# The block inverse of a gated delta rule: larger blocks on VectorE, fewer product levels on TensorE

## The chip, the core and the metric

The kernel runs on one core of one Trainium2 chip. The time is that of one execution on the device, in microseconds, as the median of three runs. A profiled execution was taken beside them; its span is the time from its first to its last instruction.

## What is computed

One layer of a hybrid decoder for 256 tokens of width 1024, all in float32:

```python
h = rms_norm(x, norm_mix)
x = x + token_mixer(h, ...)      # w_in, gated delta rule and mLSTM, w_up_*, gates, w_out
h = rms_norm(x, norm_ffn)
x = x + moe_ffn(h, ...)          # top 4 of 32 experts, clamped SwiGLU
out = rms_norm(x, norm_final)
```

The change is in the gated delta rule, with 4 heads of width 128. The reference solves in chunks of 64 tokens; the kernel takes chunks of 128, so 4 heads x 2 chunks make 8 systems:

```python
lower = where(strict, einsum("id,jd->ij", kb, k) * decay, 0.0)
sol = triangular_solve(lower + eye, rhs, lower=True, unit_diagonal=True)
u_local, w_state = sol[..., :dv], sol[..., dv:]
```

The kernel does not solve, it forms the inverse of each unit triangular 128x128 matrix (lower + eye) and multiplies with it.

## The kernel before

The mixer comes first, the experts (MoE) behind it. SyncE issues nearly all weight transfers. Into a ring of places it fetches first 24 pieces of w_in, 1 MB each, then 4 pieces of w_up and 4 of w_out, each when TensorE has finished with the piece that lay there (piece_done), and then 192 pieces of 2 MB of expert weights, each when one of ten places is free (double_done).

TensorE runs a list written out by hand. `proj(j)` multiplies piece j of w_in with the turned input (32 records in the trace, since a float32 product is two records) into bank 6 or 7 by turns. Between the proj calls stand small products of the two mixer branches. Pieces 0 to 9 go through a causal convolution, `conv(j)` on VectorE, which ends in conv_done; proj(j + 2) waits for that, since it writes the same bank. Piece 10 and those behind it are taken by ScalarE (proj_taken). Each of the engines works its list in its own order and waits on semaphores; the function `link` on VectorE makes the next instruction wait for the one just issued.

The inverse is made so. VectorE forms `lt` (the transposed strict triangle, one 128x128 block for each system, 8 side by side) and signals lt_ready. GpSimd then copies the diagonal blocks of size BASE x BASE to device memory (base_in_copy) and from there back so that each block lies within one partition: with BASE = 16 these are 64 blocks on 64 partitions. VectorE inverts them column by column, all at once, with two instructions a column (`solve_base`), and writes the inverse and its transpose (base_out). GpSimd brings both back through device memory into the diagonals of `inv` and `invT`, 128x128 blocks filled with zeros before (base_loaded). Then come three levels, for blocks of 16, 32 and 64, each of which joins two inverted blocks into one of twice the size. For a level VectorE makes `ltm`, `lt` times a mask that keeps (with the sign changed) only the blocks that the level needs (`mask_level`); TensorE multiplies it with `inv` (`level_t1`), VectorE copies the result to `t1`, TensorE forms P and Q (`level_pq`: invT with t1, t1 with invT), and VectorE adds them to `inv` and `invT` (`level_dve`). The last level leaves P out, as only `invT` is used behind it.

Around this, VectorE's list is: conv(8), solve_base, conv(9), four products into `pt` (pt_ready; the mLSTM weights), mask_level(0), three casts of the expert bias `bgu`, four products of v with beta into `vb` (vb_ready), two subtractions and more casts for the bias, one product into `kd0` (kd_ready), then mlstm_rows (which writes `om`, a part of `hn`, and signals ml_sums_taken) and the levels. TensorE's is: proj(8), proj(9), the mLSTM products of k and q, proj(10), proj(11), the transposes of v, proj(12), a wait for vb_ready, the transposes of k, proj(13), the mLSTM sums, proj(14), a wait for kd_ready, and from there the levels' batches, one between each two proj calls up to proj(20). Then come the rest of the mixer, the router and the experts.

Of the kernel before, what the change touches and what calls it, by code (L numbers as in the profile page):

```python
# [24 lines left out]
ALU = mybir.AluOpType  # L25
# [3 lines left out]
P = 128  # L29
# [5 lines left out]
HALF = 512  # L35
# [8 lines left out]
def decoder_layer(nc, x, norm_mix, w_in, gdn_conv, gdn_a_log, gdn_dt_bias, gdn_norm, ml_conv,  # L44
# [5 lines left out]
    H = gdn_a_log.shape[1]  # L50
    DH = gdn_norm.shape[1]
    T = S // P
# [47 lines left out]
    for g in range(N_GROUPS):  # L100
        a, b = GROUPS[g]
# [20 lines left out]
    with ExitStack() as ctx:  # L122
# [5 lines left out]
        def sem(name):  # L128
            if name not in sems:
                sems[name] = ctx.enter_context(nc.semaphore(name))  # L130
            return sems[name]
# [9 lines left out]
        def mixer_only(n):  # L141
            at_early[0] += n
            assert at_early[0] <= 2 * PIECE
            return early[:, at_early[0] - n:at_early[0]]
# [3 lines left out]
        hn = sb("hn", [P, T, D])  # L148
# [12 lines left out]
        lt = head4(late[3])  # L161
        ltm = sb("ltm", [P, H, T, P])
        inv, invT = head4(late[4]), head4(late[5])
        t1 = head4(late[6])
# [12 lines left out]
        triu = mixer_only(P)  # L177
        striu = sb("striu", [P, P])
        ones = sb("ones", [P, P])
        BASE = 16  # L180
        NB = P // BASE
        LEVELS = [16, 32, 64]
        level = mixer_only(len(LEVELS) * P).rearrange("p (m i) -> p m i", i=P)
        prm = sb("prm", [96, P])
        prmT = sb("prmT", [P, 96])
        ffn_rows = sb("ffn_rows", [P, KC])
        base_in = mixer_only(BASE * BASE)[0:NB * H * T, :].rearrange("q (p f) -> q p f", p=BASE)
        base_out = mixer_only(2 * BASE * BASE)[0:NB * H * T, :].rearrange("q (i r c) -> q i r c", i=2, r=BASE)
        base_step = mixer_only(BASE * BASE // 4)[0:NB * H * T, :]
        base_in_copy = nc.dram_tensor("base_in_copy", [NB, H * T, BASE, BASE], F32).ap()  # L190
        base_out_copy = nc.dram_tensor("base_out_copy", [NB, H * T, 2, BASE, BASE], F32).ap()
# [335 lines left out]
                    pool.dma_start(diagonal(v, b), base_out_copy[b, :, i].rearrange("a r c -> r a c")).then_inc(sem("base_loaded"), 16)  # L527

        TABLES = 4


        @block.tensor
        def _(pe):
            def proj(j):

                dst = B[6 + j % 2]
                landed(pe, j)
                if 2 <= j <= CONV_PIECES + 1:
                    pe.wait_ge(sem("conv_done"), 2 * (j - 1))
                if j >= CONV_PIECES + 2:  # L540
                    pe.wait_ge(sem("proj_taken"), j - 1 - CONV_PIECES)
                w = slot3(j % RING, KC)
                for c in range(2):
                    for k in range(KC):
                        if NAT_FIRST <= j < GATE_FIRST:
                            lhs, rhs = hT[:, k, c * P:(c + 1) * P], w[:, k, :]
                        else:
                            lhs, rhs = w[:, k, c * P:(c + 1) * P], hT[:, k, :]
                        mm = pe.matmul(dst[:, c * S:(c + 1) * S], lhs, rhs, start=(k == 0), stop=(k == KC - 1))  # L549
                mm.then_inc(sem("piece_done"), 1)  # L550
# [8 lines left out]
            def per_head(banks, signal, product):  # L559

                for h in range(H):
                    for t in range(T):
                        i = h * T + t
                        lhs, rhs = product(h, t)
                        mm = pe.matmul(B[banks[i // 4]][:, (i % 4) * P:(i % 4 + 1) * P], lhs, rhs, start=True, stop=True)  # L565
                        if i % 4 == 3:
                            mm.then_inc(sem(signal), 1)
# [87 lines left out]
            def level_t1(m):  # L655
                pe.wait_ge(sem("level_ready"), m + 1)
                per_head((0, 1), "t1_done", lambda h, t: (ltm[:, h, t, :], inv[:, h, t, :]))

            def level_pq(m):
                pe.wait_ge(sem("t1_ready"), m + 1)  # L660
                if m < len(LEVELS) - 1:
                    per_head((2, 3), "p_done", lambda h, t: (invT[:, h, t, :], t1[:, h, t, :]))
                per_head((4, 5), "q_done", lambda h, t: (t1[:, h, t, :], invT[:, h, t, :]))

            proj(9)

# [30 lines left out]
            mm.then_inc(sem("ml_sums_done"), 1)  # L697
            proj(14)
            pe.wait_ge(sem("kd_ready"), 1)
            pe.wait_ge(sem("base_loaded"), 16 + 16 * 2 * NB)  # L700
            level_t1(0)
            proj(15)
            pe.wait_ge(sem("ml_sums_taken"), 1)
            level_pq(0)
            proj(16)
            level_t1(1)
            proj(17)
            level_pq(1)
            proj(18)
            level_t1(2)  # L710
            proj(19)
            level_pq(2)
            proj(20)

            pe.wait_ge(sem("om_ready"), 1)
            pe.wait_ge(sem("inv_ready"), 2)
            transposes([om[:, t, h * P:(h + 1) * P] for h in range(H) for t in range(T)], (2, 3), "om_turned")
            proj(21)
            pe.wait_ge(sem("inv_ready"), 3)
            chunk_products(0, "u0_done", lambda h: (invT[:, h, 0, :], vb[:, h, 0, :]))  # L720
            proj(22)
            pe.wait_ge(sem("u0_ready"), 1)
# [358 lines left out]
        def _(dve):  # L1081
            steps = [0]

            def link(ins):

                steps[0] += 1
                ins.then_inc(sem("dve_step"), 1)
                dve.wait_ge(sem("dve_step"), steps[0])
# [146 lines left out]
            def mask_level(m):  # L1235
                dve.tensor_tensor(m8, l8, bc(level[:, m, :].unsqueeze(1), [P, H * T, P]), ALU.mult).then_inc(sem("level_ready"), 1)
# [12 lines left out]
            link(dve.tensor_tensor(v, v, bc(triu[:, :].unsqueeze(1).unsqueeze(1), [P, H, 2, P]), ALU.mult))  # L1249
            conv(8)  # L1250

            def solve_base():

                lower = base_out[:, 0]
                link(dve.memset(base_out[:, :, :, :], 0.0))
                link(dve.memset(base_out[:, 0].rearrange("q r c -> q (r c)")[:, 0:BASE * BASE:BASE + 1], 1.0))
                dve.wait_ge(sem("base_loaded"), 16)
                for j in range(BASE - 1):
                    shape = [NB * H * T, BASE - 1 - j, j + 1]
                    step = base_step[:, 0:shape[1] * shape[2]].rearrange("q (r c) -> q r c", c=j + 1)  # L1260
                    link(dve.tensor_tensor(step, bc(base_in[:, j, j + 1:BASE].unsqueeze(2), shape),
                                           bc(lower[:, j:j + 1, 0:j + 1], shape), ALU.mult))
                    v = lower[:, j + 1:BASE, 0:j + 1]
                    link(dve.tensor_tensor(v, v, step, ALU.subtract))
                dve.tensor_copy(base_out[:, 1], lower.rearrange("q r c -> q c r")).then_inc(sem("base_solved"), 1)

            solve_base()
            conv(9)
            for h in range(H):
                dve.wait_ge(sem("ml_kq_done"), h + 1)  # L1270
                w = pt[:, h, :, :].rearrange("p b i -> p (b i)")
                dve.scalar_tensor_tensor(out=w, in0=B[2 + h][:, 0:3 * P], scalar=QS, in1=w, op0=ALU.mult,
                                         op1=ALU.mult).then_inc(sem("pt_ready"), 1)
# [6 lines left out]
            def level_dve(m):  # L1280
                for b in range(2):
                    dve.wait_ge(sem("t1_done"), 2 * m + b + 1)
                    ins = dve.tensor_copy(t18[:, b * HALF:(b + 1) * HALF], B[b])
                    if b == 0:
                        link(ins)
                ins.then_inc(sem("t1_ready"), 1)
                if m < len(LEVELS) - 1:
                    for b in range(2):
                        dve.wait_ge(sem("p_done"), 2 * m + b + 1)
                        v = invf[:, b * HALF:(b + 1) * HALF]  # L1290
                        link(dve.tensor_tensor(v, v, B[2 + b], ALU.add))
                for b in range(2):
                    dve.wait_ge(sem("q_done"), 2 * m + b + 1)
                    v = invTf[:, b * HALF:(b + 1) * HALF]
                    ins = dve.tensor_tensor(v, v, B[4 + b], ALU.add)
                    if b == 0:
                        link(ins)
                ins.then_inc(sem("inv_ready"), 1)
                if m < len(LEVELS) - 1:
                    dve.wait_ge(sem("inv_ready"), m + 1)  # L1300
                    mask_level(m + 1)

            def split_bias(part):

# [47 lines left out]
            def head_norm(o, scratch, t, col):  # L1352
# [2 lines left out]
                link(dve.tensor_tensor(scratch, v, v, ALU.mult))  # L1355
                link(dve.tensor_reduce(ss[:, col:col + H], scratch.rearrange("p (h i) -> p h i", h=H), AX.X, ALU.add))

            mlstm_rows()
            dve.wait_ge(sem("base_loaded"), 16 + 16 * 2 * NB)
            level_dve(0)  # L1360
            dve.wait_ge(sem("ml_sums_taken"), 1)
            for t in range(T):
                head_norm(om, scr, t, t * H)
            dve.tensor_scalar(ss[:, :], ss[:, :], 1.0 / DH, NORM_EPS, ALU.mult, ALU.add).then_inc(sem("ml_ms_ready"), 1)
            level_dve(1)
            dve.wait_ge(sem("ml_root"), 1)
            dve.wait_ge(sem("tail_params"), 16 * 5)

# [12 lines left out]
            dve.wait_ge(sem("proj_taken"), 6)  # L1381
            for t in range(T):
                gated(om, t, mnorm[:, :].rearrange("p (h i) -> p h i", h=H), mo_s, "om_ready", t == T - 1)
            level_dve(2)
            for b in range(2):
                dve.wait_ge(sem("om_turned"), b + 1)
                ins = dve.tensor_copy(cvm[:, 2 * b:2 * b + 2, :].rearrange("p h i -> p (h i)"), B[2 + b])
# [578 lines left out]
```

## Time and profile before

| what | us |
|---|---|
| median of 3 runs | 1230.27 |
| lowest and highest | 1226.4, 1232.22 |
| the profiled execution, its own time | 1226.06 |
| its span | 1223.8 |
| TensorE busy | 1158.8 |
| VectorE busy | 310.6 |
| ScalarE busy | 128.8 |

How to read it: the share of busy time is a mean over a mixer of about 300 us and an expert part of about 900 us that are limited by different things. The chain of waits follows back from the last instruction what released it. A row of a timeline is a run of like instructions of an engine: when it starts, how long it lasts, how many there are, and in square brackets how long the engine had been idle and who released it. The records of TensorE overlap a little in a timeline; the chain gives the time from start to start.

### The profile page before, as it was taken

How to read it: one execution, taken by the hardware profiler on the slowest of the kernel's cores; microseconds unless marked ns; L12 is line 12 of the kernel's file. 1: busy time of each engine (PE TensorE's matmuls, PEld its weight loads, DVE VectorE, ACT ScalarE, POOL GpSimd, SP SyncE). 2: the span in 40 equal slices, each digit the busy share in tenths (PEclk: the TensorE clock that was granted, in tenths of full speed). 3: DMA queues.
4: the chain of work that ended last, by engine and by line, in shares of the span. 5: the costliest groups of instructions: out<-in, count | busy, mean ns of one | idle time of the engine just before them, and what ended most of it. 6: DMA issues, size and time to landing. Idle time of an engine off the chain costs nothing.

```text
span 1223.8 us, 13499 instructions
## 1 busy us (share of the span) xinstructions
PE 1158.8 (95%) x5701; PEld 598.0 (49%) x5701; DVE 310.6 (25%) x705; ACT 128.8 (11%) x216; POOL 21.3 (2%) x57
## 2 busy tenths in 40 slices
PE   8989999999999999999989898999999998899996
PEld 7878998876434343433424342434434343334342
DVE  2688432345321120201102020202112020202021
ACT  3551101001000000000000000000000000000001
POOL 1003000000000000000000000000000000000000
PEclk9999999999999999999999999999999999999999
DMA  9944334385999999999999999999999999999994
GB/s 257 383 129 142 111 103 138 110 372 211 381 428 417 428 428 428 428 427 428 427 428 427 428 427 428 427 428 427 427 427 428 428 428 428 428 427 428 428 420 194
DMA packets 63644, 443.21 MB, mean 362 GB/s; under 512 B 8772, under 2 KB 33968, under 8 KB 38016
## 3 DMA queue, kind: packets, MB, share of 16 engines
q1 hardware_dynamic: 57968, 438.38, 86.9%
q10 hardware_dynamic: 4416, 1.99, 0.7%
q0 software_dynamic: 1200, 1.98, 0.5%
q8 instruction: 46, 0.75, 0.2%
q14 instruction: 14, 0.11, 0.0%
HBM read 441.07 MB, written 1.26 MB: 361 GB/s over the span
## 4 chain that ended last, share of the span: by engine, by line
PE 62%; DMA 32%; DVE 3%; SPq 1%; issue 1%; ACT 1%; POOL 0%; ACTq 0%; DVEq 0%
DMA ring<-in_w_down 30%; PE bank L844 22%; PE bank L887 13%; PE bank L549 11%; PE bank L824 3%; PE bank L780 2%; PE bank L926 2%; PE bank L565 1%; SPq L439 1%; PE bank L750 1%; PE bank L739 1%; PE bank L836 1%; DMA ring<-rows_copy 1%; PE bank L901 1%; PE bank L572 1%
## 5 line engine op out<-in xcount | busy, mean ns | idle before, releaser
L844 PE MATMUL bank<-ring,cvg 128*64 128x512 f32 x2112 | 461.9, 593 | 9.5 <-DMA ring<-in_w_gate_up 9.2
L844 PEld LDWEIGHTS bank<-ring,cvg 128*64 128x64 f32 x2112 | 151.3, 137 | 300.8 <-issue 274.5
L887 PE MATMUL bank<-ring,cvg 128*64 128x512 f32 x1024 | 236.5, 618 | 29.4 <-DMA ring<-in_w_down 29.4
L1516 DVE TENSOR_SCALAR cvm<-bank 128x512 f32<-128x512 f32 x33 | 22.8, 692 | 651.0 <-PE bank L844 651.0
L549 PE MATMUL bank<-ring 128*128 128x256 f32 x768 | 169.7, 380 | 4.1 <-DVE cvm L1154 4.1
L887 PEld LDWEIGHTS bank<-ring,cvg 128*64 128x64 f32 x1024 | 80.0, 142 | 183.7 <-issue 183.7
L549 PEld LDWEIGHTS bank<-ring 128*128 128x128 f32 x768 | 144.4, 190 | 23.5 <-ACT ring L1826 3.5
L1896 ACT ACTIVATE cvm<-cvm 128x512 f32<-128x512 f32 x33 | 20.8, 629 | 497.4 <-DVE cvm L1516 497.4
L824 PEld LDWEIGHTS bank<-ltm,hn 128*128 128x128 f32 x544 | 66.6, 196 | 7.3 <-issue 7.1
L824 PE MATMUL bank<-ltm,hn 128*128 128x128 f32 x544 | 66.9, 281 | 0.0
L926 PE MATMUL bank<-vb,ltm 128*128 128x512 f32 x128 | 57.7, 593 | 0.0
L1905 ACT ACTIVATE vb<-bank 128x512 f32<-128x512 f32 x32 | 17.4, 594 | 244.3 <-PE bank L887 244.3
L1506 DVE TENSOR_TENSOR cvg<-bank,ffn_rows 128x512 f32<-128x512 f32 x34 | 23.4, 691 | 63.3 <-PE bank L824 63.2
L926 PEld LDWEIGHTS bank<-vb,ltm 128*128 128x128 f32 x128 | 23.2, 192 | 23.8 <-issue 23.8
L1900 ACT ACTIVATE cvg<-bank 128x512 f32<-128x512 f32 x32 | 18.9, 589 | 99.2 <-PE bank L911 99.2
L780 PE MATMUL bank<-ring 128*128 128x512 f32 x64 | 28.0, 593 | 0.0
L911 PEld LDWEIGHTS bank<-ident,cvg 128*128 128x128 f32 x132 | 18.4, 207 | 13.4 <-issue 13.0
L1521 DVE SCALAR_TENSOR_TENSOR cvm<-cvm 128x512 f32<-128x512 f32 x33 | 22.9, 693 | 4.2 <-DVE cvm L1517 0.9
L1525 DVE TENSOR_TENSOR cvg<-cvm 128x512 f32<-128x512 f32 x33 | 22.8, 692 | 1.1
L911 PE MATMUL bank<-ident,cvg 128*128 128x128 f32 x132 | 23.0, 296 | 0.0
L1517 DVE TENSOR_SCALAR cvm<-bank 128x512 f32<-128x512 f32 x33 | 22.5, 680 | 0.0
L836 PE MATMUL bank<-bgu,picked 96*64 96x512 bf16 x132 | 20.4, 386 | 0.0
(328 smaller groups left out, 550.8 us busy)
## 6 DMA issues: line engine op xcount, KB each, us to landing
ring<-in_w_gate_up SPq DMA_DIRECT2D x128, 2048.0 KB, 31.5
ring<-in_w_down SPq DMA_DIRECT2D x58, 2048.0 KB, 35.0
ring<-in_w_in SPq DMA_DIRECT2D x24, 1024.0 KB, 6.7
ring<-in_w_down SPq DMA_DIRECT2D x12, 1024.0 KB, 34.0
ring<-in_w_out SPq DMA_DIRECT2D x4, 1024.0 KB, 4.9
ring<-in_w_up_ml SPq DMA_DIRECT2D x2, 1024.0 KB, 5.1
ring<-in_w_up_gdn SPq DMA_DIRECT2D x2, 1024.0 KB, 5.0
xs<-in_x SPq DMA_DIRECT2D x2, 512.0 KB, 4.4
```

Of the source, the lines that this page charges most:

```text
L549: mm = pe.matmul(dst[:, c * S:(c + 1) * S], lhs, rhs, start=(k == 0), stop=(k == KC - 1))
L780: return pe.matmul(B[2 * t + n], gate_g[:, kk, t * P:(t + 1) * P], slot3((OUT_FIRST + i) % RING, 2)[:, k, n * HALF:(n + 1) * HALF], start= ...
L824: mm = pe.matmul(B[6 + b][:, (k % 4) * P:(k % 4 + 1) * P], by_row[:, k // 2, k % 2, :], onehot[:, t, :], start=(t == 0), stop=(t == T - 1))
L836: pe.matmul(B[4 + half][side * SLOTS:(side + 1) * SLOTS, :], picked[:, e, :], bgu[:, at:at + HALF], start=True, stop=False, skip_group_che ...
L844: mm = pe.matmul(B[4 + half][side * SLOTS:(side + 1) * SLOTS, :], xT[:, k, e * SLOTS:(e + 1) * SLOTS], w[:, (k % 2) * PIECE + at:(k % 2) * ...
L887: mm = pe.matmul(B[6 + half][e * SLOTS:(e + 1) * SLOTS, :], actT[:, e, at:at + SLOTS], by_block(double(of[e]), 4)[:, j, half * HALF:(half ...
L911: mm = pe.transpose(B[to][:, c * P:(c + 1) * P], by_row[:, c, :], ident[:, :])
L926: mm = pe.matmul(B[2 * t + half], scat[:, t, :], ysb[:, half * HALF:(half + 1) * HALF], start=False, stop=False, skip_group_check=True)
L1506: dve.tensor_tensor(xT[:, 4 * b:4 * b + 4, :], B[6 + b].rearrange("p (k s) -> p k s", k=4), bc(ffn_rows[:, 4 * b:4 * b + 4].unsqueeze(2), ...
L1516: dve.tensor_scalar(g2, both[:, :, :, 0], SWIGLU_LIMIT, None, ALU.min).then_inc(sem("glu_g_ready"), 1)
L1521: dve.scalar_tensor_tensor(out=glu_u, in0=glu_u, scalar=1.0, in1=glu_g, op0=ALU.add, op1=ALU.mult).then_inc(sem("glu_u_ready"), 1)
L1525: dve.tensor_tensor(act[:, e, :], glu_u, glu_s, ALU.mult).then_inc(sem("act_ready"), 1)
```

## The change

The diagonal blocks are now 32x32, so there are 32 of them on 32 partitions with 31 columns to work; the working arrays base_out and base_in lie in `hn`, which is free there. Only the level for blocks of 32 stays as it was, with its P and Q. The last level, for blocks of 64, is written as 64x64 quarters: the lower left quarter is `lt` times `inv` with 64 rows and 64 columns, without a mask, and its Q goes with a factor of -1 straight into a quarter of `invT`. On VectorE, conv(9) is put between columns 11 and 12 of the solve. On TensorE, proj(15) and proj(16) stand ahead of the first level. VectorE waits for base_loaded ahead of mlstm_rows. GpSimd issues 4 copies out and 8 back instead of 8 and 16.

```diff
-        BASE = 16
+        BASE = 32
-        LEVELS = [16, 32, 64]
+        LEVELS = [32]
-        base_in = mixer_only(BASE * BASE)[...]
-        base_out = mixer_only(2 * BASE * BASE)[...]
+        base_out = hn[0:NB * H * T, :, :].rearrange("q i (r c) -> q i r c", r=BASE)
+        base_in = base_out[:, 1]
...
             def level_pq(m):
                 pe.wait_ge(sem("t1_ready"), m + 1)
-                if m < len(LEVELS) - 1:
-                    per_head((2, 3), "p_done", lambda h, t: (invT[:, h, t, :], t1[:, h, t, :]))
+                per_head((2, 3), "p_done", lambda h, t: (invT[:, h, t, :], t1[:, h, t, :]))
                 per_head((4, 5), "q_done", lambda h, t: (t1[:, h, t, :], invT[:, h, t, :]))
+            def last_t1():
+                pe.wait_ge(sem("inv_ready"), len(LEVELS))
+                for i in range(H * T):
+                    h, t = i // T, i % T
+                    mm = pe.matmul(B[0][UPPER, i * HP:(i + 1) * HP], lt[LOWER, h, t, UPPER], inv[LOWER, h, t, LOWER],
+                                   start=True, stop=True)
+                mm.then_inc(sem("t1_done"), 1)
+            def last_q():
+                pe.wait_ge(sem("t1_ready"), len(LEVELS) + 1)
+                for i in range(H * T):
+                    h, t = i // T, i % T
+                    mm = pe.matmul(B[4][LOWER, i * HP:(i + 1) * HP], t1[UPPER, h, t, LOWER], invT[UPPER, h, t, UPPER],
+                                   start=True, stop=True)
+                mm.then_inc(sem("q_done"), 1)
...
             pe.wait_ge(sem("kd_ready"), 1)
+            proj(15)
+            proj(16)
             pe.wait_ge(sem("base_loaded"), 16 + 16 * 2 * NB)
             level_t1(0)
-            proj(15)
+            proj(17)
             pe.wait_ge(sem("ml_sums_taken"), 1)
             level_pq(0)
-            proj(16)
-            level_t1(1)
...
             proj(18)
-            level_t1(2)
+            last_t1()
             proj(19)
-            level_pq(2)
+            last_q()
             proj(20)
...
-            solve_base()
+            open_base()
+            solve_base(0, 12)
             conv(9)
+            solve_base(12, BASE - 1)
+            dve.tensor_copy(base_out[:, 1], lower.rearrange("q r c -> q c r")).then_inc(sem("base_solved"), 1)
...
+            def last_level():
+                side = lambda v, rows, cols: v.rearrange("p h t i -> p (h t) i")[rows, :, cols]
+                turned = B[0].rearrange("p (a i) -> p a i", i=HP)[UPPER, :, :]
+                dve.wait_ge(sem("t1_done"), 2 * len(LEVELS) + 1)
+                dve.tensor_copy(side(t1, UPPER, LOWER), turned).then_inc(sem("t1_ready"), 1)
+                dve.wait_ge(sem("q_done"), 2 * len(LEVELS) + 1)
+                dve.tensor_scalar(side(invT, LOWER, UPPER), B[4].rearrange("p (a i) -> p a i", i=HP)[LOWER, :, :], -1.0, None,
+                                  ALU.mult).then_inc(sem("inv_ready"), 1)
...
+            dve.wait_ge(sem("base_loaded"), 16 + 16 * 2 * NB)
             mlstm_rows()
-            dve.wait_ge(sem("base_loaded"), 16 + 16 * 2 * NB)
-            level_dve(0)
...
-            level_dve(1)
+            level_dve(0)
...
-            level_dve(2)
+            last_level()
```

VectorE's list from the end of the solve on, before (an instruction reads: line, operation, what it writes from what, size; L1264 is the subtraction of the solve, L1154 conv(9), L1272 pt, L1236 the mask, L1307 the casts, L1325 vb):

```order
L1264 TENSOR_TENSOR ring<-ring 64x15
L1265 COPY ring<-ring 64x256
L1154 SCALAR_TENSOR_TENSOR cvg<-bank,prmT,cvg 128x255
...
L1154 SCALAR_TENSOR_TENSOR cvg<-bank,prmT,cvg 128x253
L1272 SCALAR_TENSOR_TENSOR ring<-bank,ring 128x384 x4
L1236 TENSOR_TENSOR ltm<-ring 128x1024
L1307 CAST bgu<-ring 32x2048 x3
L1325 TENSOR_TENSOR vb<-bank,rowsrc 128x256 x4
L1315 TENSOR_TENSOR ring<-ring,bgu 32x2048 x2
L1331 TENSOR_TENSOR kd<-bank,ex 128x512
```

And after, where the same lines are L1284, L1290, L1170, L1294, L1252, L1335 and L1353; the first row is the last one of column 11:

```order
L1284 TENSOR_TENSOR hn<-hn,ring 32x20x12
L1170 SCALAR_TENSOR_TENSOR cvg<-bank,prmT,cvg 128x255
...
L1170 SCALAR_TENSOR_TENSOR cvg<-bank,prmT,cvg 128x253
L1281 TENSOR_TENSOR ring<-hn 32x247
...
L1284 TENSOR_TENSOR hn<-hn,ring 32x31
L1290 COPY hn<-hn 32x1024
L1294 SCALAR_TENSOR_TENSOR ring<-bank,ring 128x384 x4
L1252 TENSOR_TENSOR ltm<-ring 128x1024
L1335 CAST bgu<-ring 32x2048 x3
L1353 TENSOR_TENSOR vb<-bank,rowsrc 128x256 x4
```

conv(9) stood behind the whole solve and stands now behind its first 12 columns; 19 columns and the copy stand between conv(9) and all that followed it.

TensorE's list from the sums of the mLSTM branch (L695) to the transposes of om, before (L549 is a proj, 16 products; L565 the levels' batches):

```order
L695 MATMUL bank<-ones,ring 128x1 x12
L549 MATMUL bank<-ring 128x256 x16
L565 MATMUL bank<-ring,ltm 128x128 x8
L549 MATMUL bank<-ring 128x256 x16
L565 MATMUL bank<-ring 128x128 x16
L549 MATMUL bank<-ring 128x256 x16
L565 MATMUL bank<-ring,ltm 128x128 x8
...
L565 MATMUL bank<-ring 128x128 x8
L549 MATMUL bank<-ring 128x256 x16
L555 MATMUL bank<-ident,hn 128x128 x8
```

And after, with L714, L551, L567 and L557 for these, L671 for last_t1 and L680 for last_q:

```order
L714 MATMUL bank<-ones,ring 128x1 x12
L551 MATMUL bank<-ring 128x256 x48
L567 MATMUL bank<-ring,ltm 128x128 x8
L551 MATMUL bank<-ring 128x256 x16
L567 MATMUL bank<-ring 128x128 x16
L551 MATMUL bank<-ring 128x256 x16
L671 MATMUL bank<-ring 64x64 x8
L551 MATMUL bank<-ring 128x256 x16
L680 MATMUL bank<-ring 64x64 x8
L551 MATMUL bank<-ring 128x256 x16
L557 MATMUL bank<-ident,hn 128x128 x8
```

The first level's batch stood behind one proj and stands behind three; of the six batches two stay, two are now of 64x64 and two are gone, and the seven proj calls are the same.

## Rows read from the trace of the kernel before

**Rows 1.** The page: span, busy time of the engines, DMA share in 40 slices (tenths).

```profile
span 1223.8 us, 13499 instructions
...
PE 1158.8 (95%) x5701; PEld 598.0 (49%) x5701; DVE 310.6 (25%) x705; ACT 128.8 (11%) x216; POOL 21.3 (2%) x57
...
DMA  9944334385999999999999999999999999999994
```

**Rows 2.** Stretches: busy PE, PEld, DVE, ACT, POOL, granted clock, DMA share, GB/s.

```profile
270.00:280.00 10.00, 10.00 (x25) 4.50 (x24) 1.96 (x6) 1.35 (x3) 0.00 (x0) 1.00 0.11 46
...
400.00:500.00 100.00, 99.37 (x490) 39.88 (x488) 16.08 (x34) 6.86 (x12) 0.00 (x0) 1.00 1.01 428
```

**Rows 3.** Waits of the DMA queue: line, releaser, us in total, times, longest.

```profile
SPq L392 <- PE bank L844: 491.4, 120, 15.5
```

**Rows 4.** The chain of waits: start, us, engine, what, line, records.

```profile
104.25 13.81 PE bank L549 x64
...
125.85 0.44 PE bank L555 x4
...
145.46 1.78 PE bank L565 x16
...
154.16 3.57 PE bank L565 x32
...
286.05 1.71 PE bank L792 x16
...
388.05 0.68 PE bank L911 x4
```

**Rows 5.** Timeline of VectorE around the solve: start, us, line, operation, shape.

```profile
99.30 0.48 DVE L1255 MEMSET ring<- 64x512 f32 x1
...
100.41 0.17 DVE L1261 TENSOR_TENSOR ring<-ring 64x15 f32<-64x15 f32 x1 [0.48 <-DMA ring<-base_in_copy]
...
107.39 0.37 DVE L1265 COPY ring<-ring 64x256 f32<-64x256 f32 x1
107.68 2.92 DVE L1154 SCALAR_TENSOR_TENSOR cvg<-bank,prmT,cvg 128x255 f32<-128x255 f32 x6
110.52 1.94 DVE L1272 SCALAR_TENSOR_TENSOR ring<-bank,ring 128x384 f32<-128x384 f32 x4
112.38 1.22 DVE L1236 TENSOR_TENSOR ltm<-ring 128x1024 f32<-128x1024 f32 x1
113.51 3.77 DVE L1307 CAST bgu<-ring 32x2048 bf16<-32x2048 f32 x3
118.64 1.42 DVE L1325 TENSOR_TENSOR vb<-bank,rowsrc 128x256 f32<-128x256 f32 x4 [1.36 <-PE bank L555]
120.09 4.60 DVE L1315 TENSOR_TENSOR ring<-ring,bgu 32x2048 f32<-32x2048 f32 x2
```

**Rows 6.** The page's groups of instructions: weight loads, busy us, mean ns, idle.

```profile
L844 PEld LDWEIGHTS bank<-ring,cvg 128*64 128x64 f32 x2112 | 151.3, 137 | 300.8 <-issue 274.5
...
L549 PEld LDWEIGHTS bank<-ring 128*128 128x128 f32 x768 | 144.4, 190 | 23.5 <-ACT ring L1826 3.5
```

**Rows 7.** GpSimd's DMA issues (timeline), and the page's row with their landing time.

```profile
94.68 0.53 POOL L519 DMA_DIRECT2D base_in_copy<-ring  x1 [1.60 <-issue]
...
125.74 1.05 POOL L527 DMA_DIRECT2D ring<-base_out_copy  x2 [3.85 <-issue]
...
ring<-base_out_copy POOLq DMA_DIRECT2D x16, 8.0 KB, 4.3
```

**Rows 8.** Timeline of TensorE: down projection batches behind a wait (in brackets).

```profile
627.89 8.78 PE L887 MATMUL bank<-ring,cvg 128*64 128x512 f32 x32 [3.60 <-DMA ring<-in_w_down]
...
745.35 7.09 PE L887 MATMUL bank<-ring,cvg 128*64 128x512 f32 x32 [2.42 <-DMA ring<-in_w_down]
...
1130.11 8.78 PE L887 MATMUL bank<-ring,cvg 128*64 128x512 f32 x32 [2.42 <-DMA ring<-in_w_down]
```

**Rows 9.** Stretch inside the first of them, columns as in rows 2.

```profile
629.00:631.00 2.00, 2.00 (x8) 0.80 (x6) 0.00 (x0) 0.00 (x0) 0.00 (x0) 0.50 1.04 442
```

More of the change, by code:

```diff
@@ L186, in decoder_layer @@
         ffn_rows = sb("ffn_rows", [P, KC])
-        base_in = mixer_only(BASE * BASE)[0:NB * H * T, :].rearrange("q (p f) -> q p f", p=BASE)
-        base_out = mixer_only(2 * BASE * BASE)[0:NB * H * T, :].rearrange("q (i r c) -> q i r c", i=2, r=BASE)
+        base_out = hn[0:NB * H * T, :, :].rearrange("q i (r c) -> q i r c", r=BASE)
+        base_in = base_out[:, 1]
         base_step = mixer_only(BASE * BASE // 4)[0:NB * H * T, :]
@@ L529, in decoder_layer @@
         TABLES = 4
+        HP = P // 2
+        LOWER, UPPER = slice(0, HP), slice(HP, P)
         @block.tensor
@@ L699, in _ @@
             pe.wait_ge(sem("kd_ready"), 1)
+            proj(15)
+            proj(16)
             pe.wait_ge(sem("base_loaded"), 16 + 16 * 2 * NB)
             level_t1(0)
-            proj(15)
+            proj(17)
             pe.wait_ge(sem("ml_sums_taken"), 1)
             level_pq(0)
-            proj(16)
-            level_t1(1)
-            proj(17)
-            level_pq(1)
             proj(18)
-            level_t1(2)
+            last_t1()
             proj(19)
-            level_pq(2)
+            last_q()
             proj(20)
             pe.wait_ge(sem("om_ready"), 1)
-            pe.wait_ge(sem("inv_ready"), 2)
             transposes([om[:, t, h * P:(h + 1) * P] for h in range(H) for t in range(T)], (2, 3), "om_turned")
             proj(21)
-            pe.wait_ge(sem("inv_ready"), 3)
+            pe.wait_ge(sem("inv_ready"), 2)
             chunk_products(0, "u0_done", lambda h: (invT[:, h, 0, :], vb[:, h, 0, :]))
@@ L1250, in _, with open_base, solve_base @@
             conv(8)
[L1252 to L1256, printed above, removed]
+            lower = base_out[:, 0]
+            def open_base():
+                link(dve.memset(lower, 0.0))
+                link(dve.memset(lower.rearrange("q r c -> q (r c)")[:, 0:BASE * BASE:BASE + 1], 1.0))
                 dve.wait_ge(sem("base_loaded"), 16)
-                for j in range(BASE - 1):
+            def solve_base(first, end):
+                for j in range(first, end):
                     shape = [NB * H * T, BASE - 1 - j, j + 1]
@@ L1264, in solve_base @@
                     link(dve.tensor_tensor(v, v, step, ALU.subtract))
-                dve.tensor_copy(base_out[:, 1], lower.rearrange("q r c -> q c r")).then_inc(sem("base_solved"), 1)
-            solve_base()
+            open_base()
+            solve_base(0, 12)
             conv(9)
+            solve_base(12, BASE - 1)
+            dve.tensor_copy(base_out[:, 1], lower.rearrange("q r c -> q c r")).then_inc(sem("base_solved"), 1)
             for h in range(H):
@@ L1286, in level_dve @@
                 ins.then_inc(sem("t1_ready"), 1)
[L1287 to L1291, printed above, removed]
+                for b in range(2):
+                    dve.wait_ge(sem("p_done"), 2 * m + b + 1)
+                    v = invf[:, b * HALF:(b + 1) * HALF]
+                    link(dve.tensor_tensor(v, v, B[2 + b], ALU.add))
                 for b in range(2):
@@ L1298, in level_dve @@
                 ins.then_inc(sem("inv_ready"), 1)
-                if m < len(LEVELS) - 1:
-                    dve.wait_ge(sem("inv_ready"), m + 1)
-                    mask_level(m + 1)
+            def last_level():
[6 more added lines that the diff above has]
+                                  ALU.mult).then_inc(sem("inv_ready"), 1)
             def split_bias(part):
```

## The prediction, made before the changed kernel ran

> **What bounds the kernel now.** I read the page's busy shares and slices first. TensorE is busy 95% of the span and VectorE 25%, and the DMA row is low in slices 3 to 8 and full from slice 11 on [rows 1]. So there are two parts. From about 310 us on the expert weights stream at 428 GB/s with a DMA share of 1.01; just before, at 270 to 280 us, the share is 0.11 [rows 2]. The DMA queue's waits say why: its expert fetches (L392) waited 491.4 us in all for TensorE's gate-up products to free a place [rows 3]. The stream is full once the first place comes free, soon after 300 us, and it then runs to the end. It can begin earlier only if TensorE begins the experts earlier. So the span is the time at which TensorE comes to the experts plus a stretch of fixed length, and a microsecond of TensorE's path in the mixer is a microsecond of the whole.
>
> The second view is the chain of waits in the mixer. From 104 us on, through all the levels of the inverse, it is TensorE alone, each batch beginning where the one before ends [rows 4]; VectorE, ScalarE and GpSimd work under that cover. There a product removed is time won, and any wait of TensorE is time lost. So the question is how close under its cover VectorE lies. Its timeline answers that [rows 5].
>
> **Products removed and added.** Before, the three levels hold 3 t1 batches of 1.78 us, 2 pairs of P and Q batches of 3.57 (one row of each, [rows 4]) and one Q batch, half a pair, 1.78: 5.34 + 7.14 + 1.78 = 14.26 us. One t1 batch and one pair stay, 5.35. New are two batches of eight 64x64 products, 16 records each. Price of a record: a 128x32 output costs 1.71 / 16 = 107 ns, hardly less than the 111 of a full one, as long as the weights have 128 columns [rows 4]. Weights of 64 columns load in 137 ns where 128 columns take 190 [rows 6], 53 ns less, which would leave 54 to 58 ns a record. So a batch is between 0.9 and 1.78 us; I take 0.9, because the loads fix the pace of the narrow record.
>
> Going from full tiles to narrow ones and back has a price too: four transposes right behind the 128*64 products (L911) take 0.68 us where four among full ones (L555) take 0.44 [rows 4]. That is 0.24 a batch. The Trainium skill ("TensorEngine Tiling (Array Packing)", Key Properties) says that changing the tiling mode drains TensorE; by that rule the two batches are dearer than their records, and the trace agrees, with those 0.24 us; free of charge they would leave the result 0.5 us lower. Sum: 2 x (0.9 + 0.24) = 2.3 us, between 1.8 and 4.0. Gain on TensorE: 14.26 - 5.35 - 2.3 = **6.6 us**, between 4.9 and 7.1.
>
> **The solve on VectorE, which the gain is paid with.** Before, columns 0 to 14 are 30 instructions on 64 partitions, from 100.41 to 107.39 us: 6.98 us. Their elements are 2 x 680 = 1360. A 1024-element two-input operation (L1236) takes 1.22 us and a 15-element one 0.17, so 1.04 ns an element [rows 5]; 1.42 us of the 6.98 is elements, and the rest is 0.185 us an instruction. After, column j has (31 - j)(j + 1) elements, twice. Columns 0 to 11: 24 x 0.185 + 3692 x 0.00104 = 8.3 us. Columns 12 to 30: 38 x 0.185 + 7220 x 0.00104 = 14.5 us. That fewer partitions are used gives nothing back: two subtractions on 32 partitions take 4.60 us for 2048 elements each (L1315), 1.1 ns an element [rows 5]. The transposed copy took 0.37 us for 256 elements; for 1024 I take 0.37 + 768 x 0.00104 = 1.17, with 0.7 (half of that rate) and 1.3 as ends.
>
> **When it starts.** conv(8) ends at 99.3. The memset (L1255) took 0.48 us for 512 elements [rows 5] and has 1024 now, some 0.4 us more, so VectorE is ready at 100.4 instead of 100.0. The blocks reached it at 100.41. GpSimd issues 4 copies instead of 8, each with twice the pieces (the number of rows moved, 1024, is the same), and it paused 1.6 us before the eighth [rows 7]; the blocks may come up to 0.5 us sooner, which gains nothing, or 1.6 later. I take 100.5.
>
> **First wait: conv(9).** It starts at 100.5 + 8.3 = 108.8 instead of 107.68 and ends at 111.75 instead of 110.6. proj(11) waits for it (same bank) and began at 111.16, the middle of the two that the chain merges at 104.25 [rows 4]. It will begin at about 111.85: **0.7 us** lost. The slack was 0.5 us, and the part ahead of it grows by 1.15.
>
> **Second wait: vb_ready.** This is the large one. Nothing moves the rest of VectorE's list, so all that stood behind conv(9) now stands behind 19 more columns. Behind the solve: 111.75 + 14.5 + 1.17 = 127.45. Then, as before, four products with pt 1.86, the mask 1.13, three casts of the bias 3.77 and four products of v with beta 1.42, together 8.15 us without a wait [rows 5]: vb_ready comes at 135.6 instead of 120.06. TensorE wants it for the four transposes of k, which began at 125.85 [rows 4] and would now be reached at 126.55. It had 5.8 us of slack and needs 15.5: TensorE stands still for **9.1 us**. Together both waits move the transposes from 125.85 to 135.7, by 9.85 us. Error: 0.02 us an instruction is 1.2 us, the late blocks 1.6, the copy 0.5.
>
> **The clock after the wait.** Six batches of 32 products of the down projection that follow waits of 2.4 to 3.6 us took about 8.7 us, the first and the last of them 8.78, where the same batch takes 7.09 [rows 8]; inside the first of them the granted clock was 0.50, that is 1.2 GHz instead of 2.4 [rows 9]. The batch of 7.09 shown had waited 2.42 us too and lost nothing [rows 8]. After a wait of 9 us I take one such loss, **1.7 us**, with 0 and 3.4 (twice) as ends. The Trainium skill ("TensorE: Matmul & The Clock Gate", Part 1) says that an idle TensorE falls to half rate and has to be busy for a while before it gets the full one back; the trace shows that for waits of this size, though not each time. Without the rule and the rows the sum would be 1.7 lower.
>
> **Other edges.** The blocks' way back to inv and invT took from 107.8 (solved) to about 130.6: the last issue at 126.3 and 4.3 us to land [rows 7]. It now starts at 127.5 and by the same length ends at about 150.5, perhaps 152, with the same 2048 rows moved. level_t1(0) stood at 145.46 and has two projections more ahead of it: 145.46 + 9.85 + 1.7 + 2 x 6.91 = 170.8. So it is hidden by 19 us; at its old place, at 157.0, it would be so by 5. mlstm_rows, which now waits for the blocks too because om shares hn with them, ends at about 154; level_pq(0) wants it at about 179.5. kd_ready comes about 5.3 us behind vb_ready (the two subtractions of 4.60 us lie between, [rows 5]), at 141, and is wanted at 157. In the last level VectorE's copy of t1 stands behind gated as before; it is one copy where there were two, against a batch that is 0.6 us shorter, so its cover stays about what it was. The two masks and the one P add that drop out of VectorE's list were hidden, so they bring nothing.
>
> **Sum.** 9.85 + 1.7 - 6.6 = +4.95 us. Made against the profiled execution: span 1223.8 to 1228.8, its time 1226.06 to 1231.0. Against the median, which lies 4.2 above the profiled time, 1230.27 + 4.95 = **1235.2 us**, 0.40% slower. About 0.5%, 6.15 us, is what a measurement of this kernel can tell from no change.
>
> **Rivals.**
> *The waits are smaller.* If an element cost half on 32 partitions, the solve would be 5.7 us shorter, the first wait gone and the second 4.05: 4.05 + 1.7 - 6.6 = -0.85, 1229.4. For it speak only the casts on 32 partitions, 3.77 us for three of 2048 elements, which have one input; against it the subtractions with two, 1.1 ns an element [rows 5]. 6%.
> *No wait at all*, the gain alone: 1230.27 - 6.6 = 1223.7. It needs vb_ready 9.85 us sooner than I work out. 4%.
> *The way back outlasts its cover*, the slower side. GpSimd paused 3.85 us before its last two issues [rows 7]; with pieces twice as large, it may pause longer. It decides from 43 us for the way back (127.5 to 170.8), where it took 23. At 50 us, TensorE waits another 6.7: 1241.9. Against it: the number of rows moved is the same. 6%.
> *The stream covers it.* If the end hung on the DMA alone, the start of the experts would not matter: 1230.3. Against it: the share of 0.11 at 270 us and the queue's waits for TensorE. 5%.
> *The forecast*, both waits and the clock: 79%. Its own ends: the gain 4.9 to 7.1, the waits 8.5 to 11.5, the clock 0 to 3.4. Not all lie at one end together: 1231.5 to 1240.5.
>
> **How the numbers follow.** Over 1236.4 (slower by 0.5%) lies somewhat under half of the forecast's case, 34 of its 79 in a hundred; with the way back it is 40%. Within 0.5%: 45 + 6 + 5, less a little for the runs' own spread of 6 us, 55%. Faster: 5%. The range of 8 in 10 takes in the smaller waits partly and leaves out the case without a wait and the worst of the way back: 1228 to 1241.5.
>
> **What would show it.** After proj(12), the first transpose of k idle for about 9 us, released by VectorE's product into vb; a granted clock near 0.5 right behind it. About 22.8 us for the solve's 62 instructions. A gap of 0.7 us before proj(11). 16 records of 64x64 in about 0.9 us plus the change of tiles. The first gate-up product about 5 us later than before, the stream from there as before. It is wrong if vb_ready comes before 127, if the experts start earlier than they did, or if TensorE waits at level_t1(0).

## The result and the profile after

The changed kernel takes 1232.46 us (median of 9 runs, 1229.83 to 1236.34) and the kernel before 1228.26 beside it (9 runs, 1226.34 to 1232.22; the 1230.27 of the prediction was the median of its first three). The ratio is 1.0032 with a 95% interval of 1.0017 to 1.0047: slower by 4.2 us, between 2.1 and 5.8. The forecast was 1235.2 us, +4.95, with a range of 1228 to 1241.5.

| what | before | after |
|---|---|---|
| profiled execution: its time, its span | 1226.06, 1223.8 | 1231.99, 1230.2 |
| TensorE busy | 1158.8 | 1156.5 |
| VectorE busy | 310.6 | 318.3 |

TensorE's timeline after, from proj(11) to the transposes of om (L551 is proj, L557 the transposes, L567 a full level batch, L671 and L680 the 64x64 batches; in brackets the idle time ahead and its releaser):

```profile
111.36 7.14 PE L551 MATMUL bank<-ring 128*128 128x256 f32 x32 [0.66 <-DVE cvg L1170]
118.34 1.04 PE L557 MATMUL bank<-ident,cvg 128*128 128x128 f32 x8
119.21 7.07 PE L551 MATMUL bank<-ring 128*128 128x256 f32 x32
134.69 1.12 PE L557 MATMUL bank<-ident,cvg 128*128 128x128 f32 x4 [8.41 <-DVE vb L1353]
135.60 9.15 PE L551 MATMUL bank<-ring 128*128 128x256 f32 x32
144.59 2.84 PE L709 MATMUL bank<-ring 128*128 128x128 f32 x24
147.26 2.74 PE L714 MATMUL bank<-ones,ring 128*128 128x1 f32 x24
149.86 22.65 PE L551 MATMUL bank<-ring 128*128 128x256 f32 x96
172.35 1.95 PE L567 MATMUL bank<-ring,ltm 128*128 128x128 f32 x16
...
191.62 1.14 PE L671 MATMUL bank<-ring 64*64 64x64 f32 x16
192.69 7.17 PE L551 MATMUL bank<-ring 128*128 128x256 f32 x32
199.80 1.14 PE L680 MATMUL bank<-ring 64*64 64x64 f32 x16
200.87 7.17 PE L551 MATMUL bank<-ring 128*128 128x256 f32 x32
207.88 1.04 PE L557 MATMUL bank<-ident,hn 128*128 128x128 f32 x8
```

The case can be read from these rows. TensorE waits 0.66 us for conv(9) ahead of proj(11), and 8.41 us for VectorE's product into vb ahead of the transposes of k; before, it had neither wait. proj(13), right behind, takes 8.99 us from start to start where 6.91 is usual. The 64x64 batches take 1.07 us from start to start, and the proj behind each takes 0.2 us more than usual (7.1 instead of 6.91 in the chain of waits). The first level's batch follows its projections with no wait, so the blocks' way back is covered.

VectorE's timeline after, the same stretch as [rows 5] (L1281 and L1284 are the two instructions of a column, L1170 conv(9), L1290 the transposed copy, L1294 pt, L1252 the mask, L1335 the casts, L1353 vb):

```profile
98.94 0.91 DVE L1272 MEMSET hn<- 32x1024 f32 x1
99.94 0.09 DVE L1273 MEMSET hn<- 32x32 f32 x1
100.06 0.18 DVE L1281 TENSOR_TENSOR ring<-hn 32x31 f32<-32x31 f32 x1
...
107.84 0.40 DVE L1284 TENSOR_TENSOR hn<-hn,ring 32x240 f32<-32x240 f32 x1
108.27 2.94 DVE L1170 SCALAR_TENSOR_TENSOR cvg<-bank,prmT,cvg 128x255 f32<-128x255 f32 x6
111.12 0.39 DVE L1281 TENSOR_TENSOR ring<-hn 32x247 f32<-32x247 f32 x1
...
125.52 1.04 DVE L1290 COPY hn<-hn 32x1024 f32<-32x1024 f32 x1
126.48 1.93 DVE L1294 SCALAR_TENSOR_TENSOR ring<-bank,ring 128x384 f32<-128x384 f32 x4
128.34 1.20 DVE L1252 TENSOR_TENSOR ltm<-ring 128x1024 f32<-128x1024 f32 x1
129.47 3.71 DVE L1335 CAST bgu<-ring 32x2048 bf16<-32x2048 f32 x3
133.22 1.42 DVE L1353 TENSOR_TENSOR vb<-bank,rowsrc 128x256 f32<-128x256 f32 x4
```

VectorE does not wait once from 98.9 to 134.6 us. The solve's two parts take 8.2 us (100.06 to 108.27) and 14.4 (111.12 to 125.52), against 6.98 for the whole solve before. vb_ready comes at 134.64 where it came at 120.06.

The granted clock around the wait (columns as in [rows 2]; the first number behind the engines' busy times is the clock):

```profile
130.00:132.00 2.00, 0.00 (x0) 0.00 (x0) 1.93 (x3) 0.00 (x0) 0.00 (x0) 0.50 0.94 350
...
136.00:138.00 2.00, 2.00 (x6) 1.61 (x5) 1.97 (x2) 0.00 (x0) 1.55 (x3) 0.50 0.08 14
138.00:140.00 2.00, 2.00 (x6) 1.58 (x6) 1.96 (x2) 0.00 (x0) 0.23 (x2) 0.55 0.17 35
140.00:142.00 2.00, 2.00 (x12) 1.74 (x11) 1.94 (x2) 0.00 (x0) 2.00 (x2) 1.00 0.00 0
...
150.00:152.00 2.00, 2.00 (x7) 1.53 (x7) 1.77 (x6) 0.00 (x0) 0.00 (x0) 0.51 0.00 0
```

During the wait the granted clock falls to 0.50, that is 1.2 GHz, and it stays there for the first 5 us of the work behind it. At 150 us it falls once more, without a wait ahead; this I had not forecast.

### The profile page after: what moved, and what is told of

Its sections match the earlier page's. It is cut to its first block, busy times and chain, and to the rows that moved or that the text cites. A ratio compares the mean times of both kernels' runs of the same rounds, so it can differ in the third digit from the quotient of the medians.

```text
span 1230.2 us, 13400 instructions
## 1 busy us (share of the span) xinstructions
PE 1156.5 (94%) x5653; PEld 593.0 (48%) x5653; DVE 318.3 (26%) x727; ACT 128.7 (10%) x216; POOL 15.1 (1%) x39
## 4 chain that ended last, share of the span: by engine, by line
PE 57%; DMA 32%; DVE 7%; SPq 2%; issue 1%; ACT 1%; POOL 0%; ACTq 0%; DVEq 0%
DMA ring<-in_w_down 30%; PE bank L860 21%; PE bank L903 13%; PE bank L551 8%; PE bank L840 2%; PE bank L796 2%; PE bank L942 2%; SPq L439 2%; PE bank L766 1%; PE bank L755 1%; DVE hn L1284 1%; PE bank L852 1%; DVE ring L1281 1%; DVE cvm L1170 1%; DVE cvg L1170 1%
## 5 line engine op out<-in xcount | busy, mean ns | idle before, releaser
L551 PE MATMUL bank<-ring 128*128 128x256 f32 x768 | 173.6, 386 | 3.9 <-DVE cvm L1170 3.3
L551 PEld LDWEIGHTS bank<-ring 128*128 128x128 f32 x768 | 147.1, 194 | 25.0 <-ACT ring L1853 2.7
```

## Experiments

### 1. vb ahead of the rest of the solve

```diff
             conv(9)
-            solve_base(12, BASE - 1)
-            dve.tensor_copy(base_out[:, 1], lower.rearrange("q r c -> q c r")).then_inc(sem("base_solved"), 1)
             for h in range(H):
...
             ins.then_inc(sem("vb_ready"), 1)
+            solve_base(12, BASE - 1)
+            dve.tensor_copy(base_out[:, 1], lower.rearrange("q r c -> q c r")).then_inc(sem("base_solved"), 1)
```

> The changed kernel with one thing moved: columns 12 to 30 of the solve and its copy stand behind the products into vb instead of ahead of pt, mask and casts. Theory (the place of vb_ready in VectorE's list costs the time): the wait of 8.4 us ahead of the transposes of k and the slow clock behind it (2.5 us) both go, so about 11 us below the changed kernel, 1221.5, that is 6.5 us below the kernel before. Rival 1 (the way back of the blocks): the solve ends at about 136 instead of 126.6 and the way back took 20 us, so the blocks are there at about 156 and the first level wants them at 159.5; if the way back is longer by more than 3 us, TensorE waits there instead and part of the gain is gone. Rival 2 (the experts' stream sets the end whatever the mixer does): the time stays at 1232.

Measured: 1220.85 us (6 runs), ratio to the kernel before 0.9948 (0.9931 to 0.9965), span 1218.2. That is 11.6 us below the changed kernel, where 11 had been expected; the two ran on different occasions, and by their ratios to the kernel before, each taken beside its own, it is 10.3 us. The four longest waits of TensorE from 95 to 320 us are now (line, releaser, us, times, longest):

```profile
PE bank L551 <- DVE cvg L1170: 0.8, 1, 0.8
PE bank L766 <- DVE cvg L1437: 0.8, 1, 0.8
PE bank L574 <- DVE ring L1465: 0.8, 1, 0.8
PE bank L755 <- ACT ring L1904: 0.8, 1, 0.8
```

The wait for vb is gone, the one for conv(9) is still there, and the other three of 0.8 us were there before too, as were two shorter ones. The work on VectorE is the same as in the changed kernel, instruction for instruction; only its order differs. So it was not the larger solve as such that cost the time, but what stood behind it. The first level's batch comes at 161.18, without a wait. VectorE's mlstm_rows, which waits for the same blocks, begins at 154.98, released by their landing, so they were there 6.2 us before TensorE wanted them: rival 1 fell. So did rival 2.

### 2. conv(9) two columns sooner

```diff
-            solve_base(0, 12)
+            solve_base(0, 10)
             conv(9)
...
-            solve_base(12, BASE - 1)
+            solve_base(10, BASE - 1)
```

> As the kernel with vb first, and conv(9) behind column 9 instead of column 11. Theory: conv(9) ends 1.7 us sooner, so the wait of 0.66 us ahead of proj(11) goes, and nothing else changes: 0.7 us below vb_first. Rival (the wait ahead of proj(11) is not conv(9)'s): it stays.

Measured: 1220.41 us, ratio 0.9950 (0.9930 to 0.9969). The wait ahead of proj(11) is gone: proj(10) and proj(11) are one row now.

```profile
103.70 13.98 PE L551 MATMUL bank<-ring 128*128 128x256 f32 x64
```

So that wait was conv(9)'s. The time is 0.4 us lower, which the runs can't tell from nothing. The same kernel again, beside variants of its own:

> The kernel vb_first_10 once more, beside its own variants on one chip: 1220.4, between 1219 and 1222. Whether the granted clock falls behind the one-column sums in its profile (it did in three of five profiles so far, for 1.7 us) is open.

It took 1220.78 us, ratio 0.9947 (0.9935 to 0.9959). This time the clock stayed full behind the sums, in the same program.

### 3. TensorE kept busy through the wait

```diff
             proj(12)
+            pe.wait_ge(sem("proj_taken"), 2)
+            keep_busy(36)
             pe.wait_ge(sem("vb_ready"), 1)
```

> The changed kernel with 36 products of the identity by itself (7.8 us, into a free bank, used by nobody) on TensorE ahead of its wait for vb_ready. Theory (2.5 us of the loss are the clock behind the wait): the transposes of k start as late as in the changed kernel, proj(13) takes 6.9 instead of 8.9 us from start to start, and the time is 2.5 us lower, about 1230. Rival (the clock costs nothing that the rest would not absorb): same time as the changed kernel. Rival (the filler delays the transposes): later by up to 0.2 us.

Measured: 1230.29 us, 2.2 below the changed kernel (2.5 expected), ratio to the kernel before 1.0020 (1.0006 to 1.0034). By the ratios the gain is 1.5 us, and the two intervals overlap, so the time alone does not show it; the rows do. The fillers (L582), the transposes and proj(13):

```profile
126.51 8.20 PE L582 MATMUL bank<-ident 128*128 128x128 f32 x72
135.09 0.65 PE L557 MATMUL bank<-ident,cvg 128*128 128x128 f32 x4 [0.38 <-DVE vb L1355]
135.58 7.07 PE L551 MATMUL bank<-ring 128*128 128x256 f32 x32
```

The transposes start at 135.09 instead of 134.69, 0.38 us after the last filler and released by vb, so the fillers did not delay them. They take 0.49 us instead of 0.91 from start to start, and proj(13) 6.91 instead of 8.99: 2.5 us, the price of the slow clock by itself. The filled kernel stays slower than the one before, so the clock was the smaller part and the 8.4 us of waiting the larger.

### 4. The quarters alone

The kernel before with LEVELS = [16, 32] and last_t1, last_q and last_level of the changed kernel in place of level_t1(2), level_pq(2) and level_dve(2); blocks of 16 as before.

> The kernel before, with its last level alone written as 64x64 quarters without a mask (blocks of 16, levels 16 and 32 as full products). Theory: two batches of 1.78 us become two of about 1.27 (1.07 and 0.2 in the next proj), so 1.0 us less than the kernel before, and no new wait. Rival (a change of tile shape costs as much as the smaller products save): no difference. Either is below what the time can tell; the start of the transposes of om and of the experts in the profile tells it.

Measured: 1227.94 us, ratio 1.0000 (0.9985 to 1.0014). In its trace, the transposes of k start at 127.40 and those of om at 201.71, 74.31 us between them; before it was 75.34 (125.69 to 201.03). So 1.03 us are gained there, as expected, but the total shows nothing.

```profile
185.45 1.14 PE L671 MATMUL bank<-ring 64*64 64x64 f32 x16
186.52 7.17 PE L551 MATMUL bank<-ring 128*128 128x256 f32 x32
193.63 1.14 PE L680 MATMUL bank<-ring 64*64 64x64 f32 x16
194.70 7.17 PE L551 MATMUL bank<-ring 128*128 128x256 f32 x32
```

A batch costs 1.07 us plus 0.2 in the proj behind it, against 1.78.

The start of the experts, the other sign that had been named, is no help: it comes at 307.50, which is 3.49 us later than before. Of that, 1.71 lie ahead of the transposes of k (0.16 of it a wait for conv(9) that was not there before), and 2.81 come behind the transposes of om, where the granted clock was 0.50 from 296 to 302 us in this profile and never below 1.00 in that of the kernel before. The same 12 products, in the router (the part that picks the experts), before and here:

```profile
295.94 1.60 PE L580 MATMUL bank<-ident 128*128 128x128 f32 x12
```

```profile
297.46 2.93 PE L582 MATMUL bank<-ident 128*128 128x128 f32 x12
```

### 5. The first level back in its old place

vb_first_10 with level_t1(0) behind proj(14), level_pq(0) behind proj(15), and proj(16) and proj(17) behind these.

> vb_first_10 with one part of the change undone: the first level's batches stand behind proj(14) and proj(15) again, as in the kernel before, with proj(16) and proj(17) behind them. Theory (the two proj calls moved ahead are what covers the blocks' way back): solved at 137, last GpSimd issue at about 149, the blocks there at about 153, while TensorE comes at about 145: a wait of 8 us and 2 us for the clock, 10 us above vb_first_10, 1230. Rival (the cover is not needed): same time.

Measured: 1229.69 us, ratio 1.0023 (1.0011 to 1.0034); 8.9 us above vb_first_10 beside it (1220.78), 10 expected.

```profile
137.96 7.15 PE L551 MATMUL bank<-ring 128*128 128x256 f32 x32
153.62 3.50 PE L567 MATMUL bank<-ring,ltm 128*128 128x128 f32 x16 [8.51 <-issue]
156.96 7.07 PE L551 MATMUL bank<-ring 128*128 128x256 f32 x32
```

The wait of 8.51 us has no releaser in the row ("issue"). VectorE's row shows what it is: mlstm_rows waits for the same blocks and begins at the same time, released by the landing of GpSimd's copies, the last two of which are issued at 150.96.

```profile
153.55 0.17 DVE L1369 COPY den<-bank 128x8 f32<-128x8 f32 x1 [5.36 <-DMA ring<-base_out_copy]
```

Behind the wait the batch takes 3.34 us from start to start instead of 1.78, a loss of 1.6 us at half clock, and the proj behind it runs at full speed:

```profile
153.00:156.00 3.00, 2.38 (x11) 2.41 (x12) 2.28 (x7) 0.00 (x0) 0.00 (x0) 0.50 0.03 6
```

So the two proj calls that the change moves ahead, 13.8 us of work, are what covers the way back once the solve ends at 137. With the solve ending at 126.6, as in the changed kernel, they were not needed: there mlstm_rows began at 150.10 without having to wait for the blocks, while the batch at its old place would have come at about 158.5 (172.35 less 13.8), an estimate from its trace.

### 6. The second fall of the clock

It came in proj(14), right behind the one-column sums (L714), in the profiles of the changed kernel, of busy_wait and of vb_first_10, and not in those of the kernel before, vb_first, quarters_alone, vb_first_10_b and level_early: 3 of 8. Two kernels change those sums. In the first they are 64 columns wide:

```diff
-                        mm = pe.matmul(B[4][:, t * H + h:t * H + h + 1], pt[:, h, t + j, :], ones[:, 0:1],
+                        mm = pe.matmul(B[4][:, (t * H + h) * 64:(t * H + h + 1) * 64], pt[:, h, t + j, :], ones[:, 0:64],
```

> vb_first_10 with the 12 one-column products of the mLSTM sums (L714) made 64 columns wide (the same sum in each column, one is read). Theory (the second fall of the clock, 1.7 us in proj(14), comes from TensorE having little to do in the one-column products, though it is busy in the rows): the fall goes, the products cost the same 2.6 us, and the time is up to 1.2 us lower than vb_first_10, about 1219.4. Rival (it follows from the wait ahead, or falls there by chance of timing): the clock is at 0.5 to 0.65 there as before, time as vb_first_10.

Measured: 1221.09 us, ratio 0.9941 (0.9929 to 0.9954). No fall in proj(14) of its profile, and the sums cost the same:

```profile
135.41 2.79 PE L714 MATMUL bank<-ones,ring 128*128 128x64 f32 x24
138.04 20.94 PE L551 MATMUL bank<-ring 128*128 128x256 f32 x96
```

In the second each one-column product stands right behind the wide one with the same weights:

```diff
                         pe.matmul(B[2 + t][:, h * P:(h + 1) * P], w, mv_s[:, j, h * DH:(h + 1) * DH],
                                   start=(j == 0), stop=(j == t))
-            for t in range(T):
-                for h in range(H):
-                    for j in range(t + 1):
-                        mm = pe.matmul(B[4][:, t * H + h:t * H + h + 1], pt[:, h, t + j, :], ones[:, 0:1],
-                                       start=(j == 0), stop=(j == t))
+                        mm = pe.matmul(B[4][:, t * H + h:t * H + h + 1], w, ones[:, 0:1],
+                                       start=(j == 0), stop=(j == t))
```

> vb_first_10 with each one-column product of the sums put right behind the 128-column product with the same weights, instead of all 12 behind all of these. Theory of little work: no stretch of only one-column products is left, so the clock stays, time about 1219.4 as with wide sums. Rival (chance of timing): as vb_first_10. In either case 24 + 24 records take 5.2 to 5.3 us together.

Measured: 1219.22 us (5 runs, 1218.53 to 1221.0), ratio 0.9937 (0.9924 to 0.9950), span 1216.7; no fall in proj(14) of its profile. It has the lowest median here, 8.2 us below the kernel before (1227.4 beside it) and by the ratios 11.7 below the changed one; its interval overlaps with that of vb_first_10. With one profile each and a fall that came in 3 of 8 of the others, neither the theory nor the rival is settled: the same program (vb_first_10) had the fall in one profile and not in the other. The ten profiles show such falls at two more places, in work that is the same in all of them: in the router, between 288 and 304 us, in five (vb_first_10_b, busy_wait and level_early, which lose 1.3 us each, quarters_alone and wide_sums, which lose 2.8), and near 68 us, behind a wait of 2.1 to 3.7 us for VectorE, in five (vb_first, vb_first_10, vb_first_10_b, level_early, woven_sums). So a profile without a fall at one place may have it at another, and a lower time of one kernel does not show which of them it was spared.

## Why the prediction was right, point by point

**What bounds the kernel.** Right, and the experiments show it. The first gate-up product starts, by the chain of waits of each kernel, at 304.01 (before), 310.86 (after), 299.67 (vb_first), 298.91 (vb_first_10) and 297.20 (woven_sums); the spans less these starts are 919.8, 919.3, 918.5, 918.6 and 919.5 us. The expert part is a stretch of fixed length, within 1.3 us, and slides with TensorE's path. The rows of the kernel before, of the changed one and of woven_sums:

```profile
304.01 13.88 PE bank L844 x64
```

```profile
310.86 3.15 PE bank L860 x13
```

```profile
297.20 13.88 PE bank L857 x64
```

**The products.** Gain forecast 6.6 us. From proj(14) to the transposes of om it was 62.72 us before (138.31 to 201.03) and is 58.02 after (149.86 to 207.88), 4.70 less; without the 1.76 us of the second fall in that stretch (three proj in 22.49 instead of 20.73) it is 6.46. A 64x64 batch was put at 1.14 with the change of tiles (0.9 and 0.24) and takes 1.27 (1.07 and 0.2): its records cost 67 ns, where 54 to 58 had been worked out.

**The solve.** Forecast 8.3 and 14.5 us, measured 8.2 and 14.4; the copy 1.17, measured 1.04. An element costs the same on 32 partitions as on 64: from 31 to 256 elements the operation on 32 partitions grows from 0.18 to 0.41 us, and from 15 to 64 that on 64 partitions from 0.17 to 0.22, about 1.0 ns an element in either case.

**The start.** I took 100.5; it was 100.06. This profile runs ahead of the one before by about 0.45 us at this point, on VectorE (conv(8) begins at 95.85 instead of 96.32) and on TensorE (proj(10) at 103.62 instead of 104.09). The blocks were there sooner than VectorE was ready, with GpSimd's read issued at 94.53 where it had been at 98.17, so what sets the start is the memset and not the blocks. In vb_first they came just last: the solve began at 101.70 after 0.22 us of waiting for them.

**The waits.** 0.7 and 9.1 us forecast, 0.66 and 8.41 measured. vb_ready came at 134.64, 0.96 us sooner than worked out: 0.44 is the start, 0.2 the solve, 0.2 the copy from start to start, 0.1 conv(9). TensorE was there 0.27 sooner too, which leaves the miss of 0.7 in the second wait. The transposes of k moved by 9.0 us instead of 9.85; about half of that difference is the earlier start of this profile, which the change did not make.

**The clock.** The mechanism was right and its size too small. From the transposes of k to the sums it is 7.34 us before (125.69 to 133.03) and 9.90 after: 2.56 instead of 1.7; experiment 3 gives 2.5 in the trace and 1.5 to 2.2 in the time. My rows [rows 8] came from waits of 2.4 to 3.6 us. The length of the wait is not the whole reason, though: behind the 8.51 us of experiment 5 the loss was 1.6 us, near the 1.7 that I had taken. What makes it 2.56 in the one and 1.6 in the other stays open. The fall in proj(14) was not in the forecast at all.

**The other edges.** All were covered, as worked out: the way back (the blocks were there by 150.10, the batch came at 172), kd_ready, mlstm_rows, the last level.

**The sum.** In the profiled executions the experts start 6.85 us later: 9.0 + 2.56 + 1.76 - 6.46 = 6.86. The medians differ by less, 4.2; the profile of the kernel before is of an execution 2.2 us below its median, with no fall of the clock in the mixer. Without the 1.76, which comes in some executions and not in others, the profile gives 5.1, the forecast gave 4.95. That is close in part because errors cancel: the waits 0.85 too long, the clock 0.86 too short. That part is luck. Of the 2.7 us between 1235.2 and 1232.46, 2.0 have nothing to do with the change: the forecast stood on a median of three runs of the kernel before, and six more runs lowered it from 1230.27 to 1228.26. The chances had put 55% on a change within 0.5%, and 0.32% is that.

**The rivals.** Smaller waits, no wait at all, a way back that outlasts its cover, and a stream that covers all: each failed in the changed kernel. The way back is a real danger, though: experiment 5 makes it happen.

## What to carry to other kernels

When an engine with much idle time is given more work, look at what stands behind that work in its list and how much slack each of these has, and not at its busy share: VectorE was busy a quarter of the span, and making one of its signals 14.6 us later cost 8.4 us of waiting. With the larger part of the solve put behind that signal the wait was gone, and +4.2 us became -6.9 (1220.85 against 1227.75 beside it; the ratio's interval is 0.9931 to 0.9965). Where a large wait can't be avoided, it can cost more than its length: both waits of more than 8 us here were followed by work at half clock (2.5 us lost behind 8.41, 1.6 behind 8.51), and fillers through the first got its 2.5 us back in the trace.

## What the runs showed of the hardware

The granted clock can fall with no wait ahead: in three of eight profiles it was near 0.5 in proj(14), behind 2.6 us of one-column products in which TensorE's row shows it busy throughout, and that cost 1.7 us. It did not fall there in the two kernels that have no such stretch, one profile each; whether that is the cause stays open. In the router it fell in five of ten profiles, behind waits of 0.64 and 0.35 us and products of 32 columns, and cost 1.3 or 2.8 us. Behind a wait of 8.41 us 2.56 us were lost, behind one of 8.51 us 1.6, and behind waits of 2.4 to 3.6 us 1.5 to 1.7 or nothing.

In the changed kernel GpSimd issued the copies of 256 rows three at a time, with pauses of about 1.8 us between, where it had issued seven of 128 rows with pauses of 3.3 to 3.9 [rows 7]:

```profile
132.90 1.77 POOL L527 DMA_DIRECT2D ring<-base_out_copy  x3 [5.53 <-DMA base_out_copy<-hn]
136.45 1.74 POOL L527 DMA_DIRECT2D ring<-base_out_copy  x3 [1.78 <-issue]
139.97 2.68 POOL L527 DMA_DIRECT2D ring<-base_out_copy  x2 [1.77 <-issue]
```

The 2048 rows of the way back took 9.8 us to issue instead of 16.2, which I had taken to be the same. Over the eight kernels with blocks of 32 it was 8.8 to 12.0 us: in four of them (level_early, vb_first_10_b, wide_sums, woven_sums) the pause ahead of the last two was 4.7 to 5.0 us. And the copy out, ahead of the way back, was waited for 5.53 us in the changed kernel, against 1.96 before, so a part of what the issues saved was lost there.
